# A transformer prologue re-ordered: where the filter's loads, layers, taps and squares stand among the modulation pieces

## The reference, cut to what matters

```python
def modulation(cond, w, b):
    m = jax.nn.silu(cond) @ w + b
    return jnp.split(m, 3, axis=-1)

def hyena_filter(L, w1, b1, w2, b2, w3, freq):
    ...
    hid = jnp.sin(freq[0].astype(f32) * (z @ w1.astype(f32) + b1.astype(f32)))
    hid = jnp.sin(freq[1].astype(f32) * (hid @ w2.astype(f32) + b2.astype(f32)))
    h = (hid @ w3.astype(f32)).reshape(L, 2, HY_WIDTH)
    deltas = jnp.abs(jnp.linspace(HY_MIN_DECAY, HY_MAX_DECAY, HY_WIDTH, dtype=f32))
    return h * jnp.exp(-t * deltas)[:, None, :]

def long_conv_bidir(u, h, bias):
    ...
    k = jnp.concatenate([h[:, 0], jnp.zeros((1, HY_WIDTH), f32), h[:0:-1, 1]], axis=0)
    k = k * lax.rsqrt(jnp.sum(k * k, axis=0, keepdims=True))
    kf = jnp.fft.rfft(k, n=2 * L, axis=0)
    ...

def first_block(...):
    ...
        sh, sc, gt = modulation(c, ada_w[l], ada_b[l])
        shc, scc, gtc = modulation(c_ctx, ada_w[l], ada_b[l])
        h = rms_norm(x, norm_pre[l]) * (1.0 + sc[:, None]) + sh[:, None]
        hc = rms_norm(xc, norm_pre[l]) * (1.0 + scc) + shc
        z = h @ w_in[l]
    ...
```

## Time and profile before

| | |
|---|---|
| time, three runs | 1905.05, 1903.53, 1900.63 us; median 1903.53 |
| profiled execution, first to last instruction | 1899.9 us (for what lies around this span no time is given; the median of the runs is 3.6 us above it) |
| busy in that span | PE 1874.5 us (99%), DVE 1337.0 (70%), ACT 1004.9 (53%), POOL 39.0 (2%) |
| read from HBM | 360.87 MB |
| first projection matmul | 41.97 us after the start of the span |

### The profile page before, as it was taken

One profiled execution on the slowest core, in us unless ns is written; L12 is line 12 of the kernel. 1 busy time (PEld: TensorE's weight loads), 2 busy tenths in 40 slices (PEclk: granted clock), 3 DMA queues, 4 the chain that ended last, 5 costly groups with the idle time before them and its releaser, 6 DMA issues.

```text
span 1899.9 us, 26256 instructions
## 1 busy us (share of the span) xinstructions
PE 1874.5 (99%) x10688; PEld 1587.0 (84%) x10688; DVE 1337.0 (70%) x1826; ACT 1004.9 (53%) x1462; POOL 39.0 (2%) x47
## 2 busy tenths in 40 slices
PE   7999999999999999999999999999999999999998
PEld 3899888999888998988788887788888888778887
DVE  5788789888789878855755566755566555786555
ACT  3465544564544655444544456554455444666444
POOL 1300000000000000000000000000000000000000
PEclk9999999999999999999999999999999999999999
DMA  9645675535676644465567754367755776536775
GB/s 364 223 147 182 222 241 195 188 124 174 221 246 198 211 156 134 155 220 187 161 219 225 225 190 144 133 210 220 228 197 181 226 226 213 182 111 197 226 230 166
DMA packets 123319, 375.17 MB, mean 197 GB/s; under 512 B 14080, under 2 KB 32640, under 8 KB 122432
## 3 DMA queue, kind: packets, MB, share of 16 engines
q1 hardware_dynamic: 118320, 352.11, 56.0%
q0 software_dynamic: 4592, 19.90, 3.0%
q10 hardware_dynamic: 288, 1.51, 0.2%
HBM read 360.87 MB, written 10.49 MB: 195 GB/s over the span
## 4 chain that ended last, share of the span: by engine, by line
PE 92%; DVE 5%; ACT 1%; DMA 1%; issue 1%; SPq 0%; DVEq 0%; ACTq 0%
PE PS L676 28%; PE PS L678 27%; PE PS L677 27%; DVE w_lo L2110 2%; PE PS L850 1%; PE PS L869 1%; DMA raw<-weights 1%; PE PS L1258 1%; ACT w_hi L1512 1%; PE PS L1091 1%; PE PS L959 1%; PE PS L1247 1%; PE PS L940 1%; PE PS L859 0%; PE PS L813 0%
## 5 line engine op out<-in xcount | busy, mean ns | idle before, releaser
L2110 DVE TENSOR_TENSOR w_lo<-raw,w_hi 128x1024 fp32r<-128x1024 f32 x600 | 731.7, 1233 | 390.9 <-ACT w_hi L1512 389.4
L1512 ACT ACTIVATE w_hi<-raw 128x1024 fp32r<-128x1024 f32 x600 | 625.3, 1057 | 446.9 <-DMA raw<-weights 443.9
L676 PE MATMUL PS<-w_hi,h_hi 128*128 128x512 f32 (+1 forms) x1280 | 494.9, 387 | 2.1 <-DVE w_lo L2110 1.3
L678 PE MATMUL PS<-w_hi,h_lo 128*128 128x512 f32 (+1 forms) x1280 | 488.4, 382 | 0.0
L677 PE MATMUL PS<-w_lo,h_hi 128*128 128x512 f32 (+1 forms) x1280 | 488.1, 381 | 0.0
L676 PEld LDWEIGHTS PS<-w_hi,h_hi 128*128 128x128 f32 x1280 | 240.7, 188 | 54.8 <-issue 5.1
L678 PEld LDWEIGHTS PS<-w_hi,h_lo 128*128 128x128 f32 x1280 | 240.7, 188 | 47.2
L677 PEld LDWEIGHTS PS<-w_lo,h_hi 128*128 128x128 f32 x1280 | 240.9, 188 | 45.5 <-issue 1.0
L676 PE MATMUL PS<-h_hi,w_hi 128*128 128x256 f32 x896 | 258.3, 288 | 0.7 <-issue 0.3
L676 PE MATMUL PS<-w_hi,g_hi 128*128 128x512 f32 (+1 forms) x656 | 257.1, 392 | 0.1
L677 PE MATMUL PS<-h_lo,w_hi 128*128 128x256 f32 x896 | 253.4, 283 | 0.0
(11 more groups left out here) (302 smaller groups left out, 1663.8 us busy)
## 6 DMA issues: line engine op xcount, KB each, us to landing
raw<-weights SPq DMA_DIRECT2D x610, 512.0 KB, 3.9
act_mem<-arena SPq DMA_DIRECT2D x144, 64.0 KB, 3.0
arena<-act_mem SPq DMA_DIRECT2D x36, 256.0 KB, 3.6
qk<-weights POOLq DMA_DIRECT2D x12, 512.0 KB, 4.2
v<-weights POOLq DMA_DIRECT2D x12, 512.0 KB, 5.1
x<-weights SPq DMA_DIRECT2D x8, 512.0 KB, 8.0
qk<-cond_in POOLq DMA_DIRECT2D x2, 1024.0 KB, 5.1
arena<-arena SPq DMA_DIRECT2D x32, 64.0 KB, 2.6
```

Of the source, the lines that this page charges most:

```text
L676: pe.matmul(dst, hi, m_hi_, start=first, stop=False, **kw)
L678: return pe.matmul(dst, lo, m_hi_, start=False, stop=last, **kw)
L1512: nc.scalar.activation(w_hi[:, r, :], raw[:, r, :], ACT.Copy).then_inc(w_hi_ready, 1)
L2110: V.tensor_tensor(w_lo[:, r, :], raw[:, r, :], f32(w_hi[:, r, :]), ALU.subtract).then_inc(w_lo_ready, 1)
```

## The change

The filter's two inputs (1.5 MB) were issued by ScalarE at the start, on a queue of its own; now SP issues them on the queue of the modulation loads, behind n1. TensorE runs the filter's second layer ahead of piece (0,2), not behind the first turn, and the taps ahead of piece (1,1), not behind it. VectorE's program follows: the second sine arguments ahead of the copy of piece (0,2), piece (1,1) between the two tap products, piece (1,2) between sum and difference, and the take of turn 1 behind these. On ScalarE a dummy Silu stands ahead of the wait for the condition's columns, and the squares of the taps stand ahead of the squares of the context, no longer behind the group copy.

```diff
                 sp.dma_start(ada_raw[ada_buf(n)], weights[n]).then_inc(ada_loaded[ada_buf(n)], 16)
+                if n == 1:
+                    sp.dma_start(fil, filter_in).then_inc(filter_loaded, 16)
+                    sp.dma_start(fconsts, filter_consts_in).then_inc(filter_loaded, 16)
@@ TensorE
             filter_hidden(0)
             modulation(0, 1)
+            filter_hidden(1)
             modulation(0, 2)
             ada_turn(0, 1)
-            filter_hidden(1)
             modulation(1, 0)
+            filter_taps(0)
             modulation(1, 1)
-            filter_taps(0)
             modulation(1, 2)
@@ ScalarE
-            act.dma_start(fil, filter_in).then_inc(filter_loaded, 16)
-            act.dma_start(fconsts, filter_consts_in).then_inc(filter_loaded, 16)
             act.wait_ge(ones_ready, 1)
+            nc.scalar.activation(x_rt[:, 0:1], eps[:, 0:1], ACT.Silu)
             act.wait_ge(cols_loaded, 16)
...
             lambdas()
+            tap_squares(0)
             squares(0, cx)
             nc.scalar.activation(x_rt[:, 0:1], eps[:, 0:1], ACT.Sqrt)
             copy_groups(0)
-            tap_squares(0)
             root(0)
@@ VectorE
             modulation(0, 1)
+            sine_args(1)
             modulation(0, 2)
             ada_take(0, 1)
-            sine_args(1)
             modulation(1, 0)
-            modulation(1, 1)
             lambdas()
-            filter_taps(0, lambda: modulation(1, 2))
-            filter_even_odd(0, lambda: ada_take(1, 1))
+            filter_taps(0, lambda: modulation(1, 1))
+            filter_even_odd(0, lambda: modulation(1, 2))
+            ada_take(1, 1)
             norm_rstd(0)
```

## The result

| | median | lowest to highest | runs |
|---|---|---|---|
| before | 1903.03 us | 1900.63 to 1905.05 | 5 |
| changed | 1909.83 us | 1908.66 to 1910.79 | 5 |

The medians are 6.8 us apart. The recorded ratio, which need not be that of the medians, is 1.0032, 95% interval [1.0021, 1.0042], or about 6.1 us: slower, and clear of the noise. A second batch gave 1.0033 [1.0020, 1.0046]. The forecast was 1906.9 us, +3.4 by its sum. The profiled span is 1908.6 us, 8.7 above that of before. The changed kernel's own spans lie 2.1 to 2.2 us under its times, so the profiled execution of before was 1 to 2 us faster than its median; that of the changed kernel, 1910.79 us, was the slowest of its five.

What follows compares the result with a forecast made beforehand. TensorE was taken as the bound from 57 us, so its first projection matmul sets the end. Terms 3.6 + 0.7 - 0.9 = +3.4 us made span 1899.9 into 1903.3, median 1906.9; range 1901.5 to 1911.5, the forecast's own 1905 to 1909.

Steps and rivals of the forecast that it cites:

- the rivals: Other outcomes: full clock from layer 2, 1903.6 us, chance 0.20; half clock twice, 1910.5, 0.20; faster, at best 1899.7, 0.10.
- What bounds it: TensorE bounds from 57 us on; whatever moves its first projection matmul (41.97 us) moves the end by as much.
- Loads: Filter inputs behind n1 at 418 GB/s: n1 lands near 6.2 us, the filter's last byte at 9.8, layer 1 1.0 earlier.
- Hidden layers: Layer 1 at 9.8 us, layer 2 at 13.95, turn from 18.0 taking 1.50, taps starting at 20.5 to 21.5, against 23.11.
- Taps: Filter taps on TensorE, clock rising 3 us into them: they end at 26.6 us, not 27.84, a gain of 1.2.
- T: End of the filter taps on TensorE: 27.84 us before, forecast 26.6.
- Behind the taps: ScalarE does tap squares, then context squares, table load, group copy: copies behind the reciprocal end 13.2 us after the taps, before 8.35.
- C: End of the two piece copies behind VectorE's reciprocal: 36.19 us before, forecast 39.8 before the clock term.
- Clock before the last pieces: TensorE's thin stretch may halve its clock for loads n12 to n15: +0.7 us, ends 0 and +1.5.
- The second rival: TensorE at 1.2 GHz through the taps and again through n12 to n15 and the spectrum: +7 us, 1910.5; chance 0.20.
- Given back: VectorE's first weight split runs free of GpSimd's sums, 1.22 us for 2.19: -0.9 us, ends 0 and -1.3.
- Offset: Median of the runs shown taken as 3.6 us above the profiled span, added to the forecast span of 1903.3.

Runs made afterwards that it cites:

- the five matmuls: Changed kernel plus five unread fp32 128x512 matmuls on TensorE, in its pause between turn 1's last piece and the norm's groups: 1908.39 us, 1.0025 to before.
- the last of the faster versions: Kernel before with taps and layer 2 moved ahead, copies early, plus two unread matmuls around piece (2,1) on TensorE: 1902.45 us, 0.9992 to before.

## Why the prediction was right or wrong, by its steps

**The direction and the mechanism behind the taps were right; the size was half, and the gain ahead of the taps was a loss.** The forecast put +3.4 us, 0.56 on no change and 0.37 on slower; 6.8 us is beyond the 3.8 us bound, so the likeliest class was wrong. The measured time lies inside the stated range of 1901.5 to 1911.5, but outside the forecast's own 1905 to 1909: it is the allowance for the rivals that holds it.

- *What bounds it*: right. Span and projection moved together, 8.7 and 8.9.
- *Loads*: mis-sized. Layer 1 was put at 9.8 by bytes at 418 GB/s; it started at 11.54 (10.33 to 11.54 over five profiles). Already n1, which has none of the moved bytes ahead of it, was used at 7.92 and not near 6.2. The stretch of 4 to 8 us ran at 312 GB/s (340 to 394 in the other four). What holds the one queue up there is open. Alone it costs nothing that the median shows; in the changed kernel, where the filter is the chain, 0.08%, with overlapping intervals.
- *Hidden layers*: the interval from layer 1 to the turn was right to 0.1 us (8.12 for 8.2), and the turn did wait for the copy behind the sine arguments. But the turn took 2.72 us, not 1.50. The 1.50 came from a row at full clock, and the sum, which priced n6 and n7 at either clock, had only that one price for the turn. Taps from 24.17, not 21.5.
- *Taps*: 5.4 for the 5.1 expected; by their length (3.65 at full) the clock rose about 3.5 us into them, for the 3 of the forecast. T is 29.6, not 26.6, so the gain of 1.2 in T was a loss of 1.7. This sum failed by 3.0 us: 1.7 of it from the loads, 1.2 from the turn.
- *Behind the taps*: right. The context's squares start at T + 5.3 as forecast, and where the changed kernel kept its clock C stands at T + 13.2, the very sum. Moved alone the tap squares cost 5.2 us by the medians, a fallen clock included, and put back they return 0.22%. One wait beneath it was not seen: with the squares back, the turn waits 2.36 us for VectorE's copy of piece (1,2), which the prediction had fall inside.
- *Clock before the last pieces*: mis-sized, and beyond its own range. I took 0.7 of a range to 1.5; C stands at T + 16.05 for T + 13.2, 2.85 us, since groups, turn and total ran at half clock too, not only the last four loads: the root itself starts at T + 12.3 for T + 10.2.
- *The second rival*: its 1910.5 is near the measured time, but in part by luck. Its condition (34 to 42 us under 0.8) was met at 0.53, but the taps did not run at half to their end, and the spectrum ran at full clock (3.68). Its sum is also wrong: taps from 21.5 all at half end at 28.8, as the step on the taps has it, not at 27.5, and with that the rival comes to +8.4 us, 1911.9.
- *Given back*: about half. The first split takes 1.22 as forecast, but from C to the projection's second matmul it is 5.5 us for 6.0, so 0.5 and not 0.9.
- *Offset*: the 3.6 us between span and median held about 1.5 us of a fast execution of before; spans lie 2.1 to 2.2 us under their times. It cancels in the forecast, which comes to the median of before plus 3.4.

The sum with the measured terms: C later by 9.4 (1.7 in T; 4.85 by the order and 2.85 by the clock behind it), less 0.5, is the 8.9 of the profile. The medians have 6.8 of it, since the profiled execution of before was shorter than its median and that of the changed kernel longer.

## What to carry to other kernels

Ahead of moving an instruction up on an in-order engine, ask what its wait then holds up: here 1.9 us of tap squares made ScalarE wait 6.2 us for their data, put off the four squares of the context, whose data were there, with the table load and the group copy behind them, and cost 5.2 us alone. Where two engines tie, every copy that a third one waits for must stay ahead of the work that nobody waits for. And a new pause on TensorE can be paid twice, once as the wait and once as the half clock behind it: in the profiles the second part is 2.0 and 2.85 us here, by the ratios 1.3 to 1.5 and not certain.

## What the runs showed of the hardware that was not expected

- At the lower clock twelve records of two-column matmuls took 2.72 us for 1.50, eight of them 1.87 for 1.05. Their twelve weight loads were busy 2.64 us in the changed kernel (from 19.65) and 1.41 before (from 29.62), 330 ns each for 191: weight loads slow down with the clock too.
- The granted clock fell inside long waits (in the changed kernel at about 34.5 us, in the wait of 4.09), but not only there: in before it fell at about 18.4 us, where TensorE was busy for 3.85 of the 4 us, and with the five matmuls it stayed up through the wait and fell at about 41 us, in the spectrum. The place differs between the profiles.
- The runs of a kernel scatter by 2 to 7 us, and the clock is only part of it. In the 96 runs of before in the four batches those with a mean granted clock of 0.995 took 1905.9 to 1908.3 us and those with 0.999 took 1901.3 to 1902.4; but in the last of the faster versions runs of one clock, 0.999, took 1900.5 to 1906.1. The record stands at 1.00 until its first fall even where the durations are those of half clock, so these means are not the whole of it.
- One DMA queue alone, with two loads and the filter's inputs in it, moved 312 GB/s from 4 to 8 us with its engines 98% busy, and 340, 377, 380 and 394 (97 to 102% busy) in the four other profiles with the same order of loads; with ScalarE's queue beside it the other nine profiles show 418 to 424. The cause was not tried.
